# Inverting 16x16 instead of 32x32 diagonal blocks on VectorE, with one more level on TensorE, in a fused attention and recurrence kernel

## What is computed

```
sa    = state @ (-kk_t)
state = state * w_t + sa (kk_t * a_t)^T + v_t k_t^T
y_t   = state @ r_t
```

## Time and profile before

| | |
|---|---|
| median of 3 runs | 1311.23 us (1308.65 to 1312.99) |
| profiled execution: time | 1311.98 us |
| profiled execution: span | 1310.2 us |
| TensorE busy, VectorE busy, ScalarE busy | 1207.4, 844.4, 627.9 us |
| granted TensorE clock, mean over the span | 0.967 |
| the inversion on VectorE, from the diagonal to the first L2510 | 127.45 to 166.16 us |
| the levels, from the first L2510 to the first L2589 | 166.16 to 198.62 us |

### The profile page before, as it was taken

One profiled execution on the slowest core, in us unless ns is written; L12 is line 12 of the kernel. 1 busy time (PEld: TensorE's weight loads), 2 busy tenths in 40 slices (PEclk: granted clock), 3 DMA queues, 4 the chain that ended last, 5 costly groups with the idle time before them and its releaser, 6 DMA issues.

```text
span 1310.2 us, 23949 instructions
## 1 busy us (share of the span) xinstructions
PE 1207.4 (92%) x9724; PEld 1159.2 (88%) x9724; DVE 844.4 (64%) x1452; ACT 627.9 (48%) x1079; POOL 197.9 (15%) x194
## 2 busy tenths in 40 slices
PE   6987789778997899999999999989999999999997
PEld 6977688577895799999999998979999999999997
DVE  5766956456675676664488755669656667877642
ACT  5766343453545564444344343543445445654442
POOL 2125431010001212120022100005100001122101
PEclk9998889888997999999999999999999999999999
DMA  7432220032342385555345542325554345755560
GB/s 253 152 117 90 95 82 17 33 113 88 125 153 71 128 269 176 177 167 168 127 135 177 172 152 79 113 98 193 163 175 161 130 145 177 241 185 186 164 192 33
DMA packets 53533, 185.78 MB, mean 142 GB/s; under 512 B 6704, under 2 KB 8880, under 8 KB 53168
## 3 DMA queue, kind: packets, MB, share of 16 engines
q1 hardware_dynamic: 52720, 180.97, 42.7%
q10 hardware_dynamic: 704, 3.29, 0.7%
HBM read 183.19 MB, written 1.05 MB: 141 GB/s over the span
## 4 chain that ended last, share of the span: by engine, by line
PE 71%; DVE 15%; ACT 9%; issue 4%; DMA 1%; POOL 0%; DVEq 0%; ACTq 0%; POOLq 0%
PE bank L2441 21%; PE bank L2444 21%; PE bank L2442 20%; DVE wl L1897 3%; ACT wh L1524 2%; PE bank L2456 1%; DVE zl L1989 1%; ACT L1501 1%; DVE sqr L1993 1%; PE bank L2465 1%; ACT scb L1770 1%; DMA cols<-vecs 1%; DVE tmp L2354 1%; DVE score L2285 1%; DVE tmp L2352 1%
## 5 line engine op out<-in xcount | busy, mean ns | idle before, releaser
L2441 PE MATMUL bank<-xh,wh 128*128 128x256 f32 (+1 forms) x2008 | 587.1, 292 | 21.7 <-DVE xl L2138 11.6
L2444 PE MATMUL bank<-xh,wl 128*128 128x256 f32 (+1 forms) x2008 | 577.0, 287 | 6.3 <-DVE wl L1897 6.3
L2442 PE MATMUL bank<-xl,wh 128*128 128x256 f32 (+1 forms) x2008 | 577.8, 288 | 0.0
L1897 DVE TENSOR_TENSOR wl<-raw,wh 128x1024 fp32r<-128x1024 f32 (+1 forms) x343 | 422.6, 1237 | 237.7 <-ACT wh L1524 236.3
L1524 ACT ACTIVATE wh<-raw 128x1024 fp32r<-128x1024 f32 (+1 forms) x343 | 356.1, 1044 | 302.9 <-PE bank L2444 290.5
L2441 PEld LDWEIGHTS bank<-xh,wh 128*128 128x128 f32 x2008 | 385.5, 192 | 31.3 <-issue 21.9
L2444 PEld LDWEIGHTS bank<-xh,wl 128*128 128x128 f32 x2008 | 387.6, 193 | 7.7 <-DVE wl L1897 7.7
L2442 PEld LDWEIGHTS bank<-xl,wh 128*128 128x128 f32 x2008 | 386.6, 193 | 0.6
L2441 PE MATMUL bank<-hh,wh 128*128 128x272 f32 (+1 forms) x352 | 100.3, 285 | 0.0
L2442 PE MATMUL bank<-hl,wh 128*128 128x272 f32 (+1 forms) x352 | 100.2, 285 | 0.0
L2444 PE MATMUL bank<-hh,wl 128*128 128x272 f32 (+1 forms) x352 | 100.2, 285 | 0.0
(11 more groups left out here) (362 smaller groups left out, 1546.7 us busy)
## 6 DMA issues: line engine op xcount, KB each, us to landing
raw<-w_ffn_gate SPq DMA_DIRECT2D x44, 512.0 KB, 3.6
raw<-w_ffn_up SPq DMA_DIRECT2D x44, 512.0 KB, 3.8
raw<-w_a_w_in SPq DMA_DIRECT2D x29, 512.0 KB, 3.5
raw<-w_ffn_down SPq DMA_DIRECT2D x32, 448.0 KB, 3.4
raw<-w_w_out SPq DMA_DIRECT2D x16, 512.0 KB, 3.5
raw<-w_b_w_in SPq DMA_DIRECT2D x16, 512.0 KB, 4.2
raw<-w_ffn_down SPq DMA_DIRECT2D x16, 512.0 KB, 3.5
raw<-w_ret SPq DMA_DIRECT2D x16, 512.0 KB, 3.5
```

The lines of the kernel that those rows point to most:

```text
L1897: v.tensor_tensor(lo[:, c], raws[n % N_RAW][:, c], hi[:, c].bitcast(F32), ALU.subtract).then_inc(*w_lo.up(n))
L2441: pe.matmul(ps, hi[:, c], x_hi(k), start=(k == 0), stop=False)
L2442: pe.matmul(ps, hi[:, c], x_lo(k), start=False, stop=False)
L2444: last = pe.matmul(ps, lo[:, c], x_hi(k), start=False, stop=(k == kt - 1))
```

## The change

1. `lane` works on the two 16x16 diagonal blocks of each 32x32 block at once (view `two16`, two to a partition), s = 1 to 14, on 2 times s times (15 - s) elements. `lanes_in` also clears the upper right 16x16 quarter.
2. A new level, `level_16`, joins each pair on TensorE: 96 products of 32x16 (`half_y`), a masked copy by ScalarE (factor `odd16`, 0 or 1 by partition), then two batches of 96 products (`half_x`), each added into its place by VectorE. `scatter_x` takes the place of ScalarE's part of `lanes_out`.
3. The small steps are tied to panels (`beside`) in place of five after each panel. `fill()` is called after each lane without a bound, after the new level's steps by two, and by two between the levels; what is left comes at the end.

```diff
@@ schedule
-            small_steps = []
-            for i in range(0, BT, 2):
-                small_steps.extend([bonus_in(i), bonus_in(i + 1), bonus_out(i), bonus_out(i + 1)])
-                small_steps.append(v_turn(i // 3, i // 2 % 2))
-            small_steps.append(v_turn(1, 1))
-            for which in range(2):
-                small_steps.extend([bk_turn(which, 0), bk_turn(which, 1)])
+            v_turns, bk_turns = ([step(c, part) for c in range(2) for part in range(2)] for step in (v_turn, bk_turn))
+            bonus = [(bonus_in(i), bonus_in(i + 1), bonus_out(i), bonus_out(i + 1)) for i in range(0, BT, 2)]
+            beside = {25: [*v_turns[0:2], *bonus[0][0:2]], 26: [*v_turns[2:4], *bonus[0][2:4]],
+                     27: [*bk_turns[0:2], *bonus[1][0:2]], 28: [*bk_turns[2:4], *bonus[1][2:4]],
+                     19: bonus[2][0:2], 21: bonus[2][2:4]}
             for p in LAYER0_LATE:
-                between.append(("a_w_in", p))
-                for _ in range(5 if p > 24 else 0):
-                    if small_steps:
-                        between.append(small_steps.pop(0))
+                between.extend([("a_w_in", p), *beside.get(p, ())])
             do("lanes_in")
-            for s in range(1, BLK - 1):
+            for s in range(1, HALF - 1):
                 do("lane", s)
-                if len(between) > 5:
-                    fill()
+                fill()
             do("lanes_out")
+            fill()
@@
+            half = level_16()
+            next(half)
+            fill(2)
+            next(half, None)
+            fill(2)
             lev = [levels(n) for n in range(3)]
             for n in (0, None, 1, 0, None, 2, 1, 0, None, 2, 1, "scatter", 0, None, 2, 1, None, 2):
                 if n is None:
-                    fill()
+                    fill(2)
...
+            fill(len(between))
             settle()
@@ vector_program, lane
-                    n = BLK - 1 - s
+                    n = HALF - 1 - s
...
+                    prod = lanes_tmp[:, 0:2 * s * n].rearrange("p (h r c) -> p h r c", h=2, r=s)
+                    v.tensor_tensor(prod, two16[:, :, 0:s, s:s + 1].broadcast_to([P, 2, s, n]),
+                                    two16[:, :, s:s + 1, s + 1:HALF].broadcast_to([P, 2, s, n]), ALU.mult).then_inc(
@@ scalar_program
+                elif kind == "half_y":
+                    b, freed = a
                     on.wait_ge(*xt_zero.past(0))
+                    on.wait_ge(*y_mm.past(16))
+                    s.activation(yy_m[:, :, 0:HALF], by_16(b), ACT.Copy, scale=tab("odd16")).then_inc(*y16_d.up(0))
@@ vector_program
+                elif kind == "half_x":
+                    two, = a
+                    for (b, _), part in zip(two, "xt"):
+                        on.wait_ge(*x_mm.past(part))
+                        dst = x_diag[:, 0:24, 0:HALF] if part == "x" else blocks[:, 0:24, HALF:BLK]
+                        v.tensor_tensor(dst, by_16(b), dst, ALU.add).then_inc(*d32.up(part))
@@ tensor_program
+                elif kind == "half_y":
+                    b, freed = a
+                    on.wait_ge(*ln_out.past("x"))
...
+                    for m in range(24):
+                        for q in quad:
+                            last = pe.matmul(by_16(b)[q, m, :], nlt_m[q, m, q], x_diag[q, m, 0:HALF], start=True, stop=True)
+                    last.then_inc(*y_mm.up(16))
+                elif kind == "half_x":
+                    two, = a
+                    on.wait_ge(*y16_d.past(0))
+                    on.wait_ge(*ln_out.past("t"))
+                    for (b, freed), part in zip(two, "xt"):
+                        after(on, freed)
+                        for m in range(24):
+                            for q in quad:
+                                if part == "x":
+                                    last = pe.matmul(by_16(b)[q, m, :], blocks[q, m, :], yy_m[q, m, 0:HALF],
+                                                     start=True, stop=True)
+                                else:
+                                    last = pe.matmul(by_16(b)[q, m, :], yy_m[q, m, 0:BLK], blocks[q, m, HALF:BLK],
+                                                     start=True, stop=True)
+                        last.then_inc(*x_mm.up(part))
```

More of the change, by code:

```diff
@@ L58 @@
 BLK = 32
+HALF = 16
 LAYER0_KEYS = [12, 7, 13, 8, 14, 9, 15, 10, 16, 11, 17] + list(range(6))
@@ L146, in const_tables @@
          "blkm": (r // HD == c // HD) / HD, "ones": np.ones((P, P)), "ones128": np.full((P, P), 1.0 / P),
-         "ones512": np.full((P, P), 1.0 / RET_DV), "mid": np.array([[MID, -MID]] * P)}
+         "ones512": np.full((P, P), 1.0 / RET_DV), "mid": np.array([[MID, -MID]] * P), "odd16": r // HALF % 2 * 1.0}
     t = np.concatenate([r, 128 + r, 128 + r], 1)
@@ L434, in build @@
         lanes_tmp, lanes_diag = zl[:, :], lanes_flat[:, 0:BLK * BLK:BLK + 1]
+        two16 = sqr_flat[:, 0:2 * HALF * (BLK + 1)].rearrange("p (h x) -> p h x", h=2)[:, :, 0:HALF * BLK].rearrange(
+            "p h (r c) -> p h r c", c=BLK)[:, :, :, 0:HALF]
         col_first = lambda a: a.rearrange("p a c -> p c a")
@@ L487, in build @@
             "keys_by_pool", "a_inv", "mod", "k_tilde", "bonus_r", "bonus_in", "bonus_lnb", "r_hat", "bonus_gated", "gate_scaled")
-        nlt_d, ln_in, ln_m, ln, ln_out, xx_d, yy_d = steps_of(
-            "inverse_by_vector", "nlt", "lanes_in", "lane_product", "lane", "lanes_out", "x", "y")
-        blk_d, xts, xt_d, ed_kept = steps_of("inverse_by_scalar", "block", "scattered", "t", "decay_end")
+        nlt_d, ln_in, ln_m, ln, ln_out, xx_d, yy_d, d32 = steps_of(
+            "inverse_by_vector", "nlt", "lanes_in", "lane_product", "lane", "lanes_out", "x", "y", "blocks_of_32")
+        blk_d, xts, xt_d, ed_kept, y16_d = steps_of("inverse_by_scalar", "block", "scattered", "t", "decay_end", "y16")
         nl_mm, y_mm, x_mm, t_mm = steps_of("inverse_by_tensor", "l", "y", "x", "t")
@@ L927, in step_y, with level_16 @@
                     bank.give(b, (yd, (c, i)))
+            def level_16():
+                b, freed = bank.take()
+                do("half_y", b, freed)
+                bank.give(b, (y16_d, 0))
+                yield
+                two = [bank.take() for _ in range(2)]
+                do("half_x", two)
+                for (b, _), part in zip(two, "xt"):
+                    bank.give(b, (d32, part))
+                do("scatter_x")
             def levels(n):
@@ L1627, in scalar_program @@
                 elif kind == "scatter":
-                    on.wait_ge(*ln_out.past("t"))
+                    on.wait_ge(*d32.past("t"))
                     for r in (2, 3):
@@ L2002, in vector_program @@
                     on.wait_ge(*lr_sig.past(BT - 1))
+                    v.memset(lanes[:, 0:HALF, HALF:BLK], 0.0)
                     v.memset(lanes_diag, 1.0).then_inc(*ln_in.up(0))
+                elif kind == "half_x":
+                    two, = a
+                    for (b, _), part in zip(two, "xt"):
+                        on.wait_ge(*x_mm.past(part))
+                        dst = x_diag[:, 0:24, 0:HALF] if part == "x" else blocks[:, 0:24, HALF:BLK]
+                        v.tensor_tensor(dst, by_16(b), dst, ALU.add).then_inc(*d32.up(part))
                 elif kind == "lanes_out":
-                    on.wait_ge(*ln.past(BLK - 2))
+                    on.wait_ge(*ln.past(HALF - 2))
                     on.wait_ge(*used.past(STREAM.index(("w_mem1", 3, 0, KT))))
@@ L2497, in tensor_program @@
                                 last.then_inc(*nl_mm.up(g))
+                elif kind == "half_y":
+                    b, freed = a
+                    on.wait_ge(*ln_out.past("x"))
+                    for g in range(6):
+                        on.wait_ge(*nlt_d.past(g))
+                    after(on, freed)
[8 more added lines that the diff above has]
+                    for (b, freed), part in zip(two, "xt"):
+                        after(on, freed)
+                        for m in range(24):
[7 more added lines that the diff above has]
+                        last.then_inc(*x_mm.up(part))
                 elif kind == "lev_y":
                     n, level, b, freed = a
-                    on.wait_ge(*(ln_out.past("x") if level == 5 else xx_d.past(n)))
+                    on.wait_ge(*(d32.past("x") if level == 5 else xx_d.past(n)))
                     if level == 6:
```

14 lines of the change are left out of this document (6 added, 8 removed).

## The result

| | before | after |
|---|---|---|
| median of 18 runs each | 1312.01 us | 1315.17 us (1311.98 to 1316.67) |
| ratio after / before | | 1.0021, 95% interval 1.0014 to 1.0029 |
| profiled execution: time, span | 1311.98, 1310.2 us | 1311.98, 1310.1 us |
| granted clock, mean | 0.967 | 0.972 |

The account below looks back on a forecast made before the run. VectorE was taken to bound the stretch up to 166.16 us, TensorE behind it; 146.9 + 7.6 + 40.3 = 194.8 against 198.62, 3.8 us less, gave 1307.4 us from 1311.23. Range 1302 to 1316.1, the forecast's own 1305.5 to 1309.5.

Parts of the forecast that it names:

- The lanes: VectorE's stretch from diagonal to first transpose: 17.5 us instead of 36.75, the transpose done at 146.9 us, 19.2 earlier.
- The pace of the products: New level's batches over four row groups: 8 ns a record from 32, taken as 10 ns at full clock.
- rival 1: New level: small products run one after another in their bank, 6.1 us a batch, 1318.9 us in all; chance 0.09.
- ScalarE's copy and signalling: Between first and second batch of the new level: a 0.49 us copy with 0.2 of signalling, 0.7 us.
- Three batches ... 2.3 us each: The new level on TensorE: 3 x 2.3 + 0.7 = 7.6 us, from 146.9 to 154.5.
- the rest on TensorE: From the new level's end to the first L2589 (`vtok,sqr`) product: 40.3 us, counted from 32.46 before.
- Panel 28: Panel behind the new level, not at full clock after idle time and small products: 4.3 us, between 2.85 and 5.2.
- the two waits inside: In the rest on TensorE: the 1.69 us scatter and the low clock behind it, costing 1.7 us, unchanged.
- Rival 2: New level: batches run as two row groups do, 3.1 to 5.2 us each, 5.7 more: 1313.1 us; chance 0.20.
- Rival 3: TensorE at full clock through panel 28 and behind the scatter, batches 1.6 us: 5.2 less, 1302.2 us; chance 0.27.
- Rival 4: VectorE's lanes cost 0.1 us more per operation than counted, 2.8 us less gain: 1310.2 us; chance 0.08.

Follow-up runs that it names:

- e6: The changed kernel with panel 28 moved ahead of the three batches, into TensorE's idle time: 1315.51 us, 1.0025 of the kernel before.
- e8: The changed kernel without the third batch, VectorE making its result by one more transpose of blocks: 1309.06 us, 0.9982 of the kernel before.
- e1: The changed kernel with the 96 products of half_y issued twice: 1321.96 us, 1.0071 of the kernel before.
- e2: The changed kernel joining halves in only 12 of the 24 matrices, 48 products left out of each batch: 1307.75 us, 0.9965 of the kernel before.
- e9: e8 with panel 28 ahead of the batches, and turns, bonus products and panel 19 between them: 1307.85 us, 0.9971 of the kernel before.
- e5: The changed kernel with panel 28 moved from behind the batches to between half_y and half_x: 1316.17 us, 1.0030 of the kernel before.

## Why the prediction was wrong

**Right.** The lanes: the transpose ends 21.9 us after the mark (145.91 - 124.05), 21.8 were forecast. The stretch of the lanes came out as forecast, 17.6 us against 17.5, in part by luck: the operations of lanes took 9.5 + 0.7 us against 9.0 counted (0.67 and 0.78 us at 88 elements beside two operations of GpSimd, 0.20 at 52), and the overlap of neighbouring records, which the sum left out, took about as much off again. TensorE did idle ahead of the batches, 4.4 us where I said some 3. The pace of the products: "from 32 ns over four groups" came true at the full clock, 1.79 us for 192 records in e6 (9.3 ns, I took 10; without the last record's own 0.19 us, as I counted in the earlier trace rows, 8.4), so rival 1, serial products in one bank, fell. The Trainium skill's restriction (TensorEngine Tiling (Array Packing), "Restrictions and Gotchas") that row tiles cannot use one bank at the same time is contradicted by that row, if it means that they take turns: four row groups in one bank go over three times as fast as one did, though on 16 columns instead of 32. The 0.7 us for ScalarE's copy and signalling was 0.76.

**The step that failed** is "Three batches ... 2.3 us each", with its sum of 7.6 us. The level took 13.1. Of the 5.5 us more, 3.65 are the two holes, and the other 1.8 is 2.76 us a batch at the low clock instead of 2.3, three times, and 0.4 at the cut ends. The two parts are not independent: with the first batch at the full clock (e6) the holes grew and the level was no shorter. I priced a batch by how fast the array takes products, and bounded it by other paces of the array. That its instructions must also arrive was in no term and in no rival. The rows could have warned me: the page's instruction queue had 77 packets for 1.26 MB, 16 KB each, and the change adds 576 records with as many weight loads, 4.5 blocks, the most instructions of any term in the sum. But in the kernel before no run of small records of this stage was long enough to meet the limit, a level 5 having 80 (16, 8 and 16 products), so its price could not be read there.

**Sized too small**: the rest on TensorE, 159.10 to 200.82, is 41.7 us against 40.3. Panel 28 took 4.65 us (4.3 counted). The `xt_all,work` products behind the scatter ran at the low clock, 1.94 us where 1.11 stood in the earlier trace rows, and the two panels behind them took 8.0 us. I had said that the two waits inside "stay as they are", the low clock behind the scatter with them; that low spell got longer.

Sum: 5.5 + 1.4 + 0.1 on the lanes is 7.0 us over the forecast stage of 69.7, and 76.8 was measured. The medians are 7.8 apart (1315.2 and 1307.4).

**The rivals.** Rival 2 gave nearly the right time (1313.1) for a wrong reason, and its upper bound, 1316.1, is the end of the stated range under which the measured time lies. It had the three batches at 4.2 us each from a pace of 16.4 to 27 ns, and they took 4.1 in the mean, (13.1 - 0.76) / 3; but the pace was 14.4 ns and the rest was waiting. That matters for what to do next: a slow pace would have asked for fewer columns or other row groups, the holes ask for fewer instructions, and that is what e8 did. Rival 3 (full clock, 5.2 us faster) did not come; e6 brought the full clock for the first batch only, and the holes took back what the batch gained. Rival 4, dearer lanes, held for 1.2 of its 2.8 us, by the groups above, without lengthening the stretch.

**Where the expected gain went.** The lanes gave TensorE its operands 19 us earlier, as counted; most of that was work moved behind, also as counted. The 3.8 us left over went, and 3.3 more: 3.65 into the two holes, 1.8 into slower batches, and 1.4 into the stretch behind, at a lower clock than counted.

What is shown and what is argued: that TensorE's holes lie a multiple of 128 records apart, whatever the line, bank or clock, is shown by e1, e2, e6 and e9. That it stands there because the next block of instructions has not come is read from the packets of the instruction queue; no run changed the supply itself.

## What to carry to other kernels

Price a run of small TensorE products twice, by the array's pace and by its instructions, and take the larger: here 128 records (256 instructions) came every 3.7 to 4.0 us, some 30 ns a record, where the array needed 9 to 14. Look for it as idle time "<-issue" that splits a group after a multiple of 128 records; putting a panel ahead or between didn't help in e5 and e6, removing records did in e8, even at the price of a 1 us operation on VectorE. A panel behind such a run also has a worth that its length does not show: without one (e5, e6) the small products behind ran at the low clock. And ask of a wait ahead of the critical engine what clock it leaves behind: one line that put a 1.7 us scatter earlier gained 2.7 us in the kernel before and 6.4 in e9 (in the changed kernel the times don't show a gain).

## What was not expected of the hardware

- TensorE's instructions arrive in 16 KB blocks of 256; in a run of small products one came every 3.7 to 4.0 us (e1, five edges in a row, low clock), and in 3.7 us at the full clock (e9). Others took 4.5 and 3.5 us (e6) and 4.8 (e9, from 150.15 to 154.90); the two longest had a panel's weights loading beside them, which no run tests. Before the first hole 356 records of the level passed in the changed kernel and 228 or 229 in e1 and e2, so some instructions are held ready; how many, and whether a block comes at a fixed pace or some time after the one before was begun, these runs don't tell. Runs of 128 small records take 1.90 us at the low clock, so the engine then stands for half the time.
- Four row groups in turn on one bank, 32x16 products: 9.3 ns a record at the full clock (1.79 us for 192, e6), 14.4 at the low one (2.76 us, changed kernel), the weight load of each included.
- The granted clock stayed at 0.50, the lower of its two levels, through the whole level of the changed kernel (TensorE busy for 8.7 of 13.1 us) and into the panel behind it, and came back to full within that panel. In e6, where no panel stood behind, it was still 0.50 over the next 7.35 us.
